# Attention on one core: VectorE's work for the compressed branch and the choice of blocks, one operation to a step over two units

## The chip, the core and the metric

The kernel runs on one core of a Trainium2 chip. The metric is the time of one execution of the whole program on the device, in microseconds (us). It is run several times and the median is taken; one further execution is recorded by the hardware profiler, and all durations below come from that one. Five engines work side by side, each through its own queue in order: PE (TensorE, matrix products, with its weight loads shown apart as PEld), DVE (VectorE), ACT (ScalarE), POOL (GpSimd) and SP (SyncE, which issues most DMAs). They wait for each other through semaphores.

## What is computed

The reference is a two-layer decoder trunk in float32 over 1024 tokens of 1024 features: a pooling mixer and a dense SwiGLU, then shared keys and values, an attention layer, and a mixture of experts. The change is in the attention alone. Its queries are taken in blocks of 128, for 16 heads in 4 groups that share keys. Each query attends three times, and the three results are added with gates:

```python
s = einsum(qblk, k_cmp) + bias          # compressed: 63 summaries of 32 keys, every 16
p_cmp = masked_softmax(s, dc >= 0)
o_cmp = einsum(p_cmp, v_cmp)
imp = einsum(p_cmp, cmp_to_slc)         # summed over a group's 4 heads: worth of each of 16 key blocks
score = where(forced, FORCED_SCORE, where(valid, imp, NEG))
_, sel = lax.top_k(score, 4)            # selected branch: the 4 best blocks of 64 keys
...                                     # window branch: the last 256 keys
return g0 * o_cmp + g1 * o_slc + g2 * o_win
```

So the compressed branch has to be done for a block of queries before the selected branch of that block can begin, because it chooses the blocks.

## The kernel before, in words

The program is a chain of phases; `attend` is one of them, and runs from about 1380 to 1895 us of the profile. Its work is cut into 8 **tiles** `i` of 128 queries, each tile into 4 **units** `u = 4 * i + g` (one for each group of heads `g`), and each unit into 8 **steps** `b` (written b0 to b7 below). Even steps are the selected branch of one of the group's 4 heads, over the `(i + 1) * 128` keys so far; odd steps are the window branch of the same head, over up to 384 keys. Nothing in the order is decided by a scheduler: each engine's program is written out by hand as loops over tiles, units and steps, and the engines meet at semaphores.

**PE** goes through `order`. For each step it makes the scores (`scores`, L1805, into one of two PSUM tiles `s_ps`, named att_s in the trace); then it does one part of the values of the unit before: `transpose_p` (L1828, L1831) turns the weights p, and `values` (L1847) multiplies them with v. `part` shares a unit's key tiles out over b2 to b7: **b0 and b1 have none**, b2 has at most one, the later ones have one or two. The part of a step comes after the scores of the step that follows. Since there are two score tiles, PE may make the scores of step n only when DVE has read those of step n - 2 (`free_scores`, on `s_sread`).

**DVE** reads each step's scores with the bias and the running minimum (`add_bias`: L1745 and L1750 in even steps of tiles 2 to 7, L1740 otherwise; att_neg_max is its result), and after each odd step makes two scale factors (`scale_of`, L1653, L1654) and weighs one window (`scale_win`, L1660). Between these stands its work for the **next** tile's compressed branch, which is all of what the change moves: `cmp_bias` (L1670) four times in unit g = 1, `cmp_max` (L1676, L1677), `cmp_scale` (L1682 to L1691), `block_scores` (L1696 to L1701) and `select_blocks` (L1709 to L1716). The places where they stand are these lines, in the body of the loop over steps:

```python
if g == 1 and b == 7:
    cmp_max(i + 1)
if g == 2 and b == 1:
    cmp_scale(i + 1)
if g == 2 and b == 4 and i + 1 >= 2:
    block_scores(i + 1)
if g == 2 and b == 6 and i + 1 >= 2:
    select_blocks(i + 1)
```

**ACT** takes the exponential of each step's scores (L1626), weighs the heads 0 and 2 of the selected branch (L1592), copies what PE has turned out of PSUM (`copy_pt`, L1586), and takes the exponential of the compressed branch (`exp_cmp`, L1608). **POOL** weighs the heads 1 and 3 (`scale_odd`, L1557), weighs the compressed branch (`scale_cmp`, L1535), and adds the choice of blocks to the bias of the two newest key tiles (`near_bias`, L1547, of which DVE's L1750 is the reader).

In the trace the tile `p_cmp` is called shared for even tiles and att_p_cmp for odd ones; `shares` is called shared too. A unit is said to start where DVE starts reading its first scores: units 2, 6, 10, 14, 18, 22 and 26 (g = 2 of tiles 0 to 6) start at 1397.69, 1442.79, 1493.25, 1552.10, 1617.27, 1689.68 and 1771.93 us.

Of the kernel before, what the change touches and what calls it, by code (L numbers as in the profile page):

```python
# [1412 lines left out]
def attend(nc, qkv, kt_dram, qt, load_q, s_q, kt, kct, vc, gates, win, cmpb, sel_const, row_valid, ident, ot_dram, first_sum, shared,  # L1413
# [12 lines left out]
    with ExitStack() as ctx:  # L1426
# [105 lines left out]
        def _(pool):  # L1532
# [27 lines left out]
            for u in range(4 * TILES):  # L1560
                i, g = divmod(u, 4)
                if u == 8:
                    near_bias(u, 0)
                    near_bias(u, 1)
                if u:
                    scale_odd(u - 1, 3)
                if g == 2 and i + 1 < TILES:
                    scale_cmp(i + 1)
                if u >= 8:
                    near_bias(u, 2)  # L1570
                    near_bias(u, 3)
                scale_odd(u, 1)
                if u >= 8 and u + 1 < 4 * TILES:
                    near_bias(u + 1, 0)
                    near_bias(u + 1, 1)
# [3 lines left out]
        def _(act):  # L1579
# [31 lines left out]
            for i in range(TILES):  # L1611
                for g in range(N_KV):
                    u = 4 * i + g
                    if g == 2 and i + 1 < TILES:
                        exp_cmp(i + 1)
                    for b in range(8):
                        k = 8 * u + b
                        if b % 2 == 0:
                            p = p_slc[u % 2][:, b // 2, 0:(i + 1) * P]
                        else:  # L1620
                            p = p_win[u % 2][:, b // 2, max(0, 2 - i) * P:3 * P]
                        act.wait_ge(s_sread, unit_step(u, b) + 1)
                        if k >= 8:

                            act.wait_ge(s_scale, k // 2 - 3)
                        act.activation(p, p, ACT.Exp, scale=-1.0, bias=neg_max[:, k % 8:k % 8 + 1],  # L1626
                                       accum_out=sums[:, k % 8:k % 8 + 1]).then_inc(s_exp, 1)
                        if b % 4 == 3:
                            scale_even(k - 3)
                        if u:  # L1630
                            values_part(u - 1, b)
# [5 lines left out]
        def _(dve):  # L1637
# [35 lines left out]
            def cmp_max(i):  # L1673
                pc = p_cmp[i % 2]
                dve.wait_ge(s_sread, cmp_step(i, 3) + 1)
                chain.step(dve.tensor_reduce(c_min[:, :], pc[:, :, :], AX.X, ALU.min))  # L1676
                dve.tensor_tensor(pc[:, :, :], pc[:, :, :], bc(c_min[:, :], NBL), ALU.subtract).then_inc(s_cready, 1)  # L1677

            def cmp_scale(i):
                pc = p_cmp[i % 2]  # L1680
                dve.wait_ge(s_cexp, i + 1)
                chain.step(dve.tensor_reduce(c_rs[:, :], pc[:, :, :], AX.X, ALU.add))  # L1682
                chain.step(dve.reciprocal(c_rs[:, :], c_rs[:, :]))
                if i == 0:

                    chain.step(dve.tensor_scalar(c_rs[:, :], c_rs[:, :], valid[:, 0:1], None, ALU.mult))
                if i >= 2:
                    chain.step(dve.tensor_tensor(shares[:, :, :], pc[:, :, :], bc(c_rs[:, :], NBL), ALU.mult))

                    dve.wait_ge(s_cscaled, i - 1)  # L1690
                dve.tensor_tensor(c_scale[i % 2][:, :], c_rs[:, :],  # L1691
# [61 lines left out]
            for g in range(N_KV):  # L1753
                cmp_bias(0, g)
            cmp_max(0)
            cmp_scale(0)
            for i in range(TILES):
                for g in range(N_KV):
                    u = 4 * i + g
                    for b in range(8):  # L1760
# [4 lines left out]
                        if i + 1 < TILES:  # L1765
                            if g == 1 and b % 2:
                                cmp_bias(i + 1, b // 2)
                            if g == 1 and b == 7:
                                cmp_max(i + 1)
                            if g == 2 and b == 1:  # L1770
                                cmp_scale(i + 1)
                            if g == 2 and b == 4 and i + 1 >= 2:
                                block_scores(i + 1)
                            if g == 2 and b == 6 and i + 1 >= 2:
                                select_blocks(i + 1)
            scale_of(8 * 4 * TILES - 2)
            scale_win(8 * 4 * TILES - 1)
# [775 lines left out]
```

## Time and profile before

| what | value |
|---|---|
| median of 3 runs | 4199.45 us (4198.1 to 4200.04) |
| the profiled execution, its own time | 4201.67 us |
| its span in the profile | 4200.1 us |
| PE busy, share of the span | 96% |
| DVE, ACT, POOL busy | 56%, 39%, 10% |
| mean granted clock of PE | 0.973 of full speed |

The span is the time between the first and the last record, so the profiled execution's own time is a little longer. Shares of busy time are means over all phases; what a change inside the attention is worth is read from the attention's own stretch, from the idle time of its engines and from what ended it. In rows of the timeline the number in square brackets is how long the engine sat idle before the row, and behind it stands what released it.

### The profile page before, as it was taken

The numbers are of one execution on the slowest core, as the hardware profiler recorded it, in microseconds if no ns is written. First come the engines' busy times: TensorE is split into PE (matmuls) and PEld (weight loads), VectorE is DVE, ScalarE is ACT, GpSimd is POOL, SyncE is SP. The second block draws the span as 40 slices with busy tenths as digits, with TensorE's granted clock in tenths as the row PEclk, the third lists the DMA queues.
The fourth block names the chain that finished last, engine by engine and source line by source line (L and its number), as shares of the span: only waits on it lengthen the run. The fifth ranks groups of instructions, "written<-read, shape, count | busy, mean of one in ns | idle before, by whom it ended". The sixth has DMA issues, their size and how long they took to land.

```text
span 4200.1 us, 63442 instructions
## 1 busy us (share of the span) xinstructions
PE 4015.1 (96%) x23002; PEld 3464.3 (82%) x23002; DVE 2363.0 (56%) x3482; ACT 1631.3 (39%) x2260; POOL 423.9 (10%) x439
## 2 busy tenths in 40 slices
PE   8999999998998899998699999999999999999998
PEld 6888888886887556556599999999999999999987
DVE  4444444445443676652455555555566666666678
ACT  3222222223342577673232332333334444444455
POOL 2000000000231243340100010010010100101010
PEclk8999999998999799999799999999999999999999
DMA  5222232233544211004333343344354545555567
GB/s 218 100 91 109 100 130 90 90 110 138 170 146 137 87 40 45 22 17 154 144 146 127 133 160 120 146 151 150 140 187 180 204 180 200 186 192 211 190 251 266
DMA packets 153671, 594.27 MB, mean 141 GB/s; under 512 B 26896, under 2 KB 54928, under 8 KB 113043
## 3 DMA queue, kind: packets, MB, share of 16 engines
q1 hardware_dynamic: 139076, 548.02, 36.1%
q0 software_dynamic: 10384, 35.14, 3.0%
q10 hardware_dynamic: 4080, 9.44, 0.6%
q8 instruction: 73, 1.20, 0.1%
q14 instruction: 58, 0.48, 0.0%
HBM read 535.76 MB, written 57.83 MB: 141 GB/s over the span
## 4 chain that ended last, share of the span: by engine, by line
PE 49%; DVE 1%; issue 0%; ACT 0%; DMA 0%; POOL 0%; DVEq 0%; POOLq 0%; ACTq 0%
PE moe_ps L443 10%; PE moe_ps L445 10%; PE moe_ps L444 10%; PE moe_ps L485 5%; PE moe_ps L486 5%; PE moe_ps L487 5%; PE moe_ps L424 1%; PE moe_ps L452 1%; PE moe_ps L453 1%; PE moe_ps L456 1%; DVE moe_yacc L364 0%; DMA moe_stage<-h_moe,moe_ids 0%; DVE moe_ht_lo L323 0%; PE moe_ps L458 0%; DVE moe_wd_lo L352 0%
## 5 line engine op out<-in xcount | busy, mean ns | idle before, releaser
L443 PE MATMUL moe_ps<-moe_ht_hi,moe_gu_hi 128*128 128x256 f32 (+4 forms) x3136 | 936.6, 299 | 1.6 <-DVE moe_ht_lo L323 1.6
L445 PE MATMUL moe_ps<-moe_ht_hi,moe_gu_lo 128*128 128x256 f32 (+4 forms) x3136 | 936.1, 298 | 0.0
L444 PE MATMUL moe_ps<-moe_ht_lo,moe_gu_hi 128*128 128x256 f32 (+4 forms) x3136 | 935.6, 298 | 0.0
L244 ACT CAST moe_gu_hi<-moe_gu_raw 128x2048 fp32r<-128x2048 f32 x226 | 431.0, 1907 | 521.3 <-PE moe_ps L445 487.8
L327 DVE TENSOR_TENSOR moe_gu_lo<-moe_gu_raw,moe_gu_hi 128x2048 fp32r<-128x2048 f32 x226 | 517.3, 2289 | 170.3 <-ACT moe_gu_hi L244 168.8
L443 PEld LDWEIGHTS moe_ps<-moe_ht_hi,moe_gu_hi 128*128 128x128 f32 x3136 | 596.2, 190 | 5.4 <-issue 1.8
L444 PEld LDWEIGHTS moe_ps<-moe_ht_lo,moe_gu_hi 128*128 128x128 f32 x3136 | 597.0, 190 | 3.5
L445 PEld LDWEIGHTS moe_ps<-moe_ht_hi,moe_gu_lo 128*128 128x128 f32 x3136 | 596.0, 190 | 0.0
L364 DVE SCALAR_TENSOR_TENSOR moe_yacc<-moe_ps,job_weights,moe_yacc 128x512 f32<-128x512 f32 x504 | 374.9, 750 | 326.8 <-PE moe_ps L487 326.8
L485 PE MATMUL moe_ps<-moe_wd_hi,moe_hid_hi 128*128 128x512 f32 x1008 | 395.8, 393 | 0.0
L486 PE MATMUL moe_ps<-moe_wd_lo,moe_hid_hi 128*128 128x512 f32 x1008 | 393.4, 390 | 0.0
L487 PE MATMUL moe_ps<-moe_wd_hi,moe_hid_lo 128*128 128x512 f32 x1008 | 392.9, 390 | 0.0
L443 PE MATMUL ffn_ps<-ffn_ht_hi,ffn_gu_hi 128*128 128x512 f32 x896 | 349.9, 391 | 1.6 <-DVE ffn_ht_lo L323 1.6
L444 PE MATMUL ffn_ps<-ffn_ht_lo,ffn_gu_hi 128*128 128x512 f32 x896 | 349.7, 390 | 0.0
L445 PE MATMUL ffn_ps<-ffn_ht_hi,ffn_gu_lo 128*128 128x512 f32 x896 | 349.5, 390 | 0.0
L367 DVE TENSOR_TENSOR ffn_yacc<-ffn_yacc,ffn_ps 128x512 f32<-128x512 f32 x224 | 153.8, 689 | 255.1 <-PE ffn_ps L487 254.9
L269 ACT CAST moe_hid_hi<-moe_hid 128x256 fp32r<-128x256 f32 (+4 forms) x196 | 84.9, 433 | 506.6 <-DVE moe_hid L342 506.6
L352 DVE TENSOR_TENSOR moe_wd_lo<-moe_wd_raw,moe_wd_hi 128x2048 fp32r<-128x2048 f32 x112 | 255.8, 2284 | 1.8 <-ACT moe_wd_hi L276 1.8
L342 DVE TENSOR_TENSOR moe_hid<-moe_act_gate,moe_ps 128x256 f32<-128x256 f32 (+5 forms) x224 | 96.9, 432 | 259.5 <-PE moe_ps L445 258.2
L2427 POOL DMA_INDIRECT out_x<-moe_yacc,job_to x18 | 28.8, 1597 | 1955.1 <-DVE moe_yacc L364 1955.1
L487 PEld LDWEIGHTS moe_ps<-moe_wd_hi,moe_hid_lo 128*128 128x128 f32 x1008 | 189.4, 188 | 40.3
L485 PEld LDWEIGHTS moe_ps<-moe_wd_hi,moe_hid_hi 128*128 128x128 f32 x1008 | 189.9, 188 | 37.2 <-DVE moe_yacc L364 1.1
(355 smaller groups left out, 6627.2 us busy)
## 6 DMA issues: line engine op xcount, KB each, us to landing
moe_gu_raw<-in_moe_wgu SPq DMA_DIRECT2D x228, 1024.0 KB, 4.9
moe_wd_raw<-in_moe_wd SPq DMA_DIRECT2D x112, 1024.0 KB, 6.7
first_gu<-in_ffn_wgu SPq DMA_DIRECT2D x58, 1024.0 KB, 4.8
ffn_wd_raw<-in_ffn_wd SPq DMA_DIRECT2D x28, 1024.0 KB, 6.8
kvq_lo<-qt SPq DMA_DIRECT2D x8, 1024.0 KB, 4.8
kt<-kt_rows SPq DMA_DIRECT2D x8, 1024.0 KB, 6.5
shared<-in_w_kvq SPq DMA_DIRECT2D x5, 1024.0 KB, 7.8
kvq_raw<-in_w_kvq SPq DMA_DIRECT2D x5, 1024.0 KB
```

The lines of the kernel that those rows point to most:

```text
L244: act.copy(gu_hi[s][:, :, :, :].rearrange("p a k c -> p (a k c)"), gu_raw[r][:, :]).then_inc(s_gu_hi, 1)
L327: dve.tensor_tensor(gu_lo[s][:, :, :, :].rearrange("p a k c -> p (a k c)"), gu_raw[r][:, :], gu_hi[s][:, :, :, :].rearrange("p a k c -> p ...
L342: dve.tensor_tensor(hid[s][:, 0:W], act_gate[s][:, 0:W], gate_ps[s][:, W:2 * W] if W == P else up_ps[s][:, 0:W], ALU.mult).then_inc(s_hid, 1)
L352: dve.tensor_tensor(wd_lo[b][:, :, :], wd_raw[b][:, :, :], wd_hi[b][:, :, :], ALU.subtract).then_inc(s_wd_lo, 1)
L364: dve.scalar_tensor_tensor(out=part, in0=y_ps[u % 4][:, :], scalar=row_weights[1][:, t:t + 1], in1=part, op0=ALU.mult, op1=ALU.add).then_i ...
L367: dve.tensor_tensor(part, part, y_ps[u % 4][:, :], ALU.add).then_inc(s_yadded, unit)
L443: pe.matmul(out[:, 0:W], gu_hi[s][:, half, k, :], ht_hi[:, k, 0:W], start=(k == 0), stop=False)
L444: pe.matmul(out[:, 0:W], gu_hi[s][:, half, k, :], ht_lo[:, k, 0:W], start=False, stop=False)
L445: last = pe.matmul(out[:, 0:W], gu_lo[s][:, half, k, :], ht_hi[:, k, 0:W], start=False, stop=(k == KT - 1))
L485: pe.matmul(out, hid_hi[b][:, a, rows], wd_hi[b][:, a, cols], start=(a == 0), stop=False)
L486: pe.matmul(out, hid_hi[b][:, a, rows], wd_lo[b][:, a, cols], start=False, stop=False)
L487: last = pe.matmul(out, hid_lo[b][:, a, rows], wd_hi[b][:, a, cols], start=False, stop=(a == GROUP - 1))
```

## The change

The number of operations stays the same. On DVE the old `cmp_max` is split into `cmp_max` (minimum) and `cmp_center` (subtraction), the old `cmp_scale` into `cmp_sums`, `cmp_shares` and `cmp_scale`, and the pieces stand at other steps of units g = 2 and g = 3. On ACT the exponential of the compressed branch stands ahead of b4 of unit g = 2 where it stood ahead of b0. On POOL its weighing stands in unit g = 3, behind `scale_odd(u, 1)`, where it stood in unit g = 2 behind `scale_odd(u - 1, 3)`.

```diff
--- before.py
+++ after.py
@@ -1564,12 +1564,12 @@
                     near_bias(u, 1)
                 if u:
                     scale_odd(u - 1, 3)
-                if g == 2 and i + 1 < TILES:
-                    scale_cmp(i + 1)
                 if u >= 8:
                     near_bias(u, 2)
                     near_bias(u, 3)
                 scale_odd(u, 1)
+                if g == 3 and i + 1 < TILES:
+                    scale_cmp(i + 1)
                 if u >= 8 and u + 1 < 4 * TILES:
                     near_bias(u + 1, 0)
                     near_bias(u + 1, 1)
@@ -1611,10 +1611,10 @@
             for i in range(TILES):
                 for g in range(N_KV):
                     u = 4 * i + g
-                    if g == 2 and i + 1 < TILES:
-                        exp_cmp(i + 1)
                     for b in range(8):
                         k = 8 * u + b
+                        if g == 2 and b == 4 and i + 1 < TILES:
+                            exp_cmp(i + 1)
                         if b % 2 == 0:
                             p = p_slc[u % 2][:, b // 2, 0:(i + 1) * P]
                         else:
@@ -1674,18 +1674,24 @@
                 pc = p_cmp[i % 2]
                 dve.wait_ge(s_sread, cmp_step(i, 3) + 1)
                 chain.step(dve.tensor_reduce(c_min[:, :], pc[:, :, :], AX.X, ALU.min))
+
+            def cmp_center(i):
+                pc = p_cmp[i % 2]
                 dve.tensor_tensor(pc[:, :, :], pc[:, :, :], bc(c_min[:, :], NBL), ALU.subtract).then_inc(s_cready, 1)
 
-            def cmp_scale(i):
-                pc = p_cmp[i % 2]
+            def cmp_sums(i):
                 dve.wait_ge(s_cexp, i + 1)
-                chain.step(dve.tensor_reduce(c_rs[:, :], pc[:, :, :], AX.X, ALU.add))
+                chain.step(dve.tensor_reduce(c_rs[:, :], p_cmp[i % 2][:, :, :], AX.X, ALU.add))
                 chain.step(dve.reciprocal(c_rs[:, :], c_rs[:, :]))
                 if i == 0:
 
                     chain.step(dve.tensor_scalar(c_rs[:, :], c_rs[:, :], valid[:, 0:1], None, ALU.mult))
+
+            def cmp_shares(i):
+                chain.step(dve.tensor_tensor(shares[:, :, :], p_cmp[i % 2][:, :, :], bc(c_rs[:, :], NBL), ALU.mult))
+
+            def cmp_scale(i):
                 if i >= 2:
-                    chain.step(dve.tensor_tensor(shares[:, :, :], pc[:, :, :], bc(c_rs[:, :], NBL), ALU.mult))
 
                     dve.wait_ge(s_cscaled, i - 1)
                 dve.tensor_tensor(c_scale[i % 2][:, :], c_rs[:, :],
@@ -1753,6 +1759,8 @@
             for g in range(N_KV):
                 cmp_bias(0, g)
             cmp_max(0)
+            cmp_center(0)
+            cmp_sums(0)
             cmp_scale(0)
             for i in range(TILES):
                 for g in range(N_KV):
@@ -1768,10 +1776,16 @@
                             if g == 1 and b == 7:
                                 cmp_max(i + 1)
                             if g == 2 and b == 1:
+                                cmp_center(i + 1)
+                            if g == 2 and b == 5:
+                                cmp_sums(i + 1)
+                            if g == 2 and b == 7 and i + 1 >= 2:
+                                cmp_shares(i + 1)
+                            if g == 3 and b == 0:
                                 cmp_scale(i + 1)
-                            if g == 2 and b == 4 and i + 1 >= 2:
+                            if g == 3 and b == 1 and i + 1 >= 2:
                                 block_scores(i + 1)
-                            if g == 2 and b == 6 and i + 1 >= 2:
+                            if g == 3 and b == 3 and i + 1 >= 2:
                                 select_blocks(i + 1)
             scale_of(8 * 4 * TILES - 2)
             scale_win(8 * 4 * TILES - 1)
```

The first place is DVE in unit 26 (tile 6, g = 2), from the end of b1 to the start of b2. Before:

```order
L1654 TENSOR_TENSOR att_scale<-gates,att_sums 128x2
L1660 TENSOR_SCALAR att_p_win1<-att_p_win1,att_scale 128x384
L1682 TENSOR_REDUCE att_c_rs<-att_p_cmp1 128x16
L1683 RECIPROCAL att_c_rs<-att_c_rs 128x16
L1688 TENSOR_TENSOR shared<-att_p_cmp1,att_c_rs 128x1024
L1691 TENSOR_TENSOR att_c_scale1<-att_c_rs,gates 128x16
L1745 ISA att_p_slc0,att_far_min<-att_sel0,att_s0 128x640
```

After the change (new line numbers: L1680 is `cmp_center`, L1751, L1756 and L1746 are the reads of `add_bias`):

```order
L1653 RECIPROCAL att_sums<-att_sums 128x2
L1654 TENSOR_TENSOR att_scale<-gates,att_sums 128x2
L1660 TENSOR_SCALAR att_p_win1<-att_p_win1,att_scale 128x384
L1680 TENSOR_TENSOR att_p_cmp1<-att_p_cmp1,att_c_min 128x1024
L1751 ISA att_p_slc0,att_far_min<-att_sel0,att_s0 128x640
```

Four operations stood between b1 and b2; now the subtraction alone stands there, which was in unit 25.

The second place is DVE in unit 27 (tile 6, g = 3), from the end of b0 to the start of b2. Before:

```order
L1750 ISA att_p_slc1,att_neg_max<-att_near0,att_s0,att_far_min 128x256
L1750 ISA att_neg_max 128x1
L1740 ISA att_p_win1,att_neg_max<-win,att_s1 128x384
L1740 ISA att_neg_max 128x1
L1653 RECIPROCAL att_sums<-att_sums 128x2
L1654 TENSOR_TENSOR att_scale<-gates,att_sums 128x2
L1660 TENSOR_SCALAR att_p_win0<-att_p_win0,att_scale 128x384
L1745 ISA att_p_slc1,att_far_min<-att_sel0,att_s0 128x640
```

After the change (L1697 is `cmp_scale`, L1702 to L1707 are `block_scores`):

```order
L1697 TENSOR_TENSOR att_c_scale1<-att_c_rs,gates 128x16
L1746 ISA att_p_win1,att_neg_max<-win,att_s1 128x384
L1746 ISA att_neg_max 128x1
L1653 RECIPROCAL att_sums<-att_sums 128x2
L1654 TENSOR_TENSOR att_scale<-gates,att_sums 128x2
L1660 TENSOR_SCALAR att_p_win0<-att_p_win0,att_scale 128x384
L1702 TENSOR_REDUCE att_group_p<-shared 128x256
L1704 TENSOR_REDUCE att_imp<-att_group_p 128x64
L1705 SCALAR_TENSOR_TENSOR att_imp<-att_group_p,att_imp 128x64
L1707 SCALAR_TENSOR_TENSOR att_imp<-att_group_p,att_imp 128x4x15
L1751 ISA att_p_slc1,att_far_min<-att_sel0,att_s0 128x640
```

Unit 27 held no work for the compressed branch; now one small product stands between b0 and b1, and the four operations of `block_scores` between b1 and b2. `select_blocks` follows behind b3.

The third place is POOL around its weighing of tile 7's compressed branch. Before:

```order
L1547 TENSOR_TENSOR att_near1<-win,att_sel0 128x256
L1557 TENSOR_SCALAR att_p_slc1<-att_p_slc1,att_scale 128x896
L1535 TENSOR_TENSOR att_p_cmp1<-att_p_cmp1,att_c_scale1 128x1024
L1547 TENSOR_TENSOR att_near0<-win,att_sel0 128x256
L1547 TENSOR_TENSOR att_near1<-win,att_sel0 128x256
L1557 TENSOR_SCALAR att_p_slc0<-att_p_slc0,att_scale 128x896
```

After the change:

```order
L1547 TENSOR_TENSOR att_near1<-win,att_sel0 128x256
L1557 TENSOR_SCALAR att_p_slc1<-att_p_slc1,att_scale 128x896
L1535 TENSOR_TENSOR att_p_cmp1<-att_p_cmp1,att_c_scale1 128x1024
L1547 TENSOR_TENSOR att_near0<-win,att_sel1 128x256
L1547 TENSOR_TENSOR att_near1<-win,att_sel1 128x256
L1557 TENSOR_SCALAR att_p_slc1<-att_p_slc1,att_scale 128x896
```

The weighing now stands right ahead of the first two `near_bias` of unit 28, and behind unit 27's own first weighing, `scale_odd(27, 1)`.

## Rows read from the trace of the kernel before

**Rows 1.** The page of the profile, its parts 1 and 2.
```profile
PE 4015.1 (96%) x23002; PEld 3464.3 (82%) x23002; DVE 2363.0 (56%) x3482; ACT 1631.3 (39%) x2260; POOL 423.9 (10%) x439
...
PEclk8999999998999799999799999999999999999999
```

**Rows 2.** Waits of PE, 1386 to 1915 us: total, times, longest.
```profile
PE att_s L1805 <- DVE att_neg_max L1750: 24.4, 22, 2.9
```

**Rows 3.** Stretches (eight units): us, busy PE, PEld, DVE, ACT, POOL, granted clock, DMA.
```profile
1397.69:1408.53 10.84, 8.29 (x36) 5.51 (x38) 6.97 (x33) 6.48 (x23) 3.29 (x3) 0.54 0.05 14
...
1442.79:1457.08 14.29, 10.39 (x54) 6.45 (x54) 13.49 (x45) 8.08 (x24) 4.06 (x3) 0.76 0.03 9
1552.10:1569.80 17.70, 14.06 (x78) 8.17 (x78) 16.29 (x54) 11.26 (x26) 7.88 (x7) 0.90 0.03 8
1617.27:1636.97 19.70, 16.14 (x94) 9.98 (x95) 17.25 (x53) 13.25 (x29) 8.53 (x7) 0.91 0.03 8
1689.68:1714.05 24.37, 20.49 (x104) 12.14 (x102) 17.16 (x53) 14.78 (x30) 9.21 (x7) 0.79 0.02 6
1714.05:1731.17 17.12, 16.49 (x104) 10.09 (x104) 9.26 (x37) 13.30 (x30) 7.36 (x6) 1.00 0.20 70
1771.93:1793.74 21.81, 17.69 (x110) 10.71 (x110) 17.73 (x52) 14.99 (x31) 9.83 (x7) 1.00 0.02 7
1793.74:1812.81 19.07, 18.48 (x114) 11.01 (x112) 9.94 (x36) 14.76 (x31) 7.94 (x6) 1.00 0.03 9
```

**Rows 4.** Timeline of unit 26, steps 0 to 2: start, length in us.
```profile
1770.43 1.22 DVE L1677 TENSOR_TENSOR att_p_cmp<-att_p_cmp,att_c_min 128x1024 f32<-128x1024 f32 x1
...
1774.13 2.75 POOL L1557 TENSOR_SCALAR att_p_slc<-att_p_slc,att_scale 128x896 f32<-128x896 f32 x1 [6.93 <-DVE att_scale L1654]
...
1774.40 1.21 DVE L1682 TENSOR_REDUCE att_c_rs<-att_p_cmp 128x16 f32<-128x1024 f32 x1
...
1775.14 0.65 PE L1847 MATMUL att_o<-att_pt,first_sum 128*64 128x256 f32 x4
...
1775.94 1.22 DVE L1688 TENSOR_TENSOR shared<-att_p_cmp,att_c_rs 128x1024 f32<-128x1024 f32 x1
...
1777.31 0.82 DVE L1745 CUSTOM_DVE_ANT_0 att_p_slc<-att_sel,att_s 128x640 f32<-128x640 f32 x1
...
1778.72 1.08 PE L1805 MATMUL att_s<-kt,kvq_lo 128*128 128x512 f32 x4 [2.93 <-DVE att_neg_max L1750]
```

**Rows 5.** Timeline of unit 27, steps 1 to 3.
```profile
1796.96 0.65 PE L1847 MATMUL att_o<-att_pt,first_sum 128*64 128x256 f32 x4
...
1797.55 0.55 DVE L1740 CUSTOM_DVE_ANT_0 att_p_win<-win,att_s 128x384 f32<-128x384 f32 x1
...
1797.68 1.09 PE L1805 MATMUL att_s<-kt,kvq_lo 128*128 128x512 f32 x4
```

**Rows 6.** Timeline of unit 26, steps 4 to 7, VectorE.
```profile
1781.33 1.97 DVE L1696 TENSOR_REDUCE att_group_p<-shared 128x256 f32<-128x1024 f32 x1
...
1784.33 0.56 DVE L1740 CUSTOM_DVE_ANT_0 att_p_win<-win,att_s 128x384 f32<-128x384 f32 x1
...
1787.37 0.22 DVE L1709 TENSOR_TENSOR att_imp<-att_imp,att_consts 128x64 f32<-128x64 f32 x1
...
1789.78 0.56 DVE L1740 CUSTOM_DVE_ANT_0 att_p_win<-win,att_s 128x384 f32<-128x384 f32 x1
```

**Rows 7.** Timeline of PE in unit 2.
```profile
1400.91 0.69 PE L1805 MATMUL att_s<-kt,kvq_lo 128*128 128x128 f32 x2 [2.21 <-DVE att_neg_max L1740]
```

**Rows 8.** Timeline of PE in unit 6.
```profile
1443.26 0.84 PE L1805 MATMUL att_s<-kt,kvq_lo 128*128 128x256 f32 x4 [1.68 <-DVE att_neg_max L1740]
...
1447.53 0.79 PE L1805 MATMUL att_s<-kt,kvq_lo 128*128 128x256 f32 x2 [3.42 <-DVE att_neg_max L1740]
```

**Rows 9.** Timeline of PE in units 10 and 11.
```profile
1505.18 0.62 PE L1805 MATMUL att_s<-kt,kvq_lo 128*128 128x384 f32 x2 [1.43 <-DVE att_neg_max L1740]
...
1511.32 0.92 PE L1805 MATMUL att_s<-kt,kvq_lo 128*128 128x384 f32 x3 [0.84 <-DVE att_neg_max L1750]
```

## The prediction

> **What bounds the kernel now.** I read the page first: PE is busy for 96% of the span and DVE for 56% [rows 1], so a DVE operation costs time only where PE has nothing else to do. The attention is such a place. The list of PE's waits there shows that the largest is for DVE's reading of the scores: 24.4 us in 22 times, the longest 2.9 us [rows 2]. The busy time by stretch says in which units that is. In units 23 and 27 (g = 3) PE is busy for 16.49 of 17.12 and 18.48 of 19.07 us; in units 22 and 26 (g = 2) for 20.49 of 24.37 and 17.69 of 21.81 us [rows 3]. PE idles about 4 us in each unit g = 2 and about 0.6 us in its neighbour g = 3, and the extra is what the compressed branch costs.
>
> The timeline of unit 26 says why. Behind b1 DVE goes through four operations, from 1774.40 to 1777.31, so it reads b2 only after them. PE ends its one key tile of values at about 1775.8, and starts the scores of b4 at 1778.72 after 2.93 us of idling, released by that read [rows 4]. Yet before this the minimum and the subtraction (1.22 us, at 1770.43) stood ahead of b0, and behind b4 and b6 `block_scores` held DVE from 1781.33 to 1784.33 and `select_blocks` from 1787.37 to 1789.78 [rows 6], and PE's waits do not grow by them. **The place decides, not the size**: from b2 on PE has one or two key tiles of values between two scores, at b0 and b1 it has none, and DVE sets the pace. Unit 27 shows how little slack there is without any insertion: PE's last value product before the scores of b4 starts at 1796.96 and is over by 1797.6, DVE has read b2 when b3's read starts at 1797.55, and the scores of b4 start at 1797.68 [rows 5]. The two arrive within 0.1 us of each other, so whatever stands behind b1 goes wholly into PE's time.
>
> **The change part by part, tiles 3 to 6 (four times).** Behind b1 of g = 2 stood 2.91 us (1774.40 to 1777.31); now the subtraction alone stands there, 1.22 us and a gap, 1.25: minus 1.66. Taking it away from ahead of b0 gives at most 0.1, since DVE already finished it (1771.65) before the first read of unit 26 at 1771.93. The sums (1.21 and a reciprocal, about 1.5 us) behind b5 and the shares (1.22) behind b7 cost nothing: they are smaller than the 3.0 and 2.4 us that the same steps hid. If that cover were gone they would cost up to 2.7. The scale (2.91 - 1.25 - 1.21 = 0.45 is reciprocal and scale together, so about 0.2) now stands behind b0 of g = 3: 0 to 0.2, I take 0.1. **`block_scores`, 3.00 us, now stands behind b1 of g = 3**, the uncovered place, and goes in whole: plus 3.0. `select_blocks`, 2.4 us, behind b3 has key tiles beside it: 0 to 0.2, in these tiles with 8 or more key tiles. Together -1.66 - 0.1 + 0.1 + 3.0 + 0.1 = **+1.45 each, +5.8**.
>
> **Tiles 0 to 2.** Tile 0 (next tile 1 chooses no blocks): the 1.25 us leave a place where short units do wait, and behind b1 1.25 stands for 1.21 + 0.45 = 1.66: -1.65, against a wait of 2.21 us [rows 7]. Tile 1: PE waited 1.68 and 3.42 us [rows 8]; -1.25 - 1.66 in unit 6, +3.0 in unit 7, and `select_blocks` finds one key tile a step, about 1.5 us of PE for a step, so +0.5: +0.6. Tile 2: DVE is full in the old unit 10, so `block_scores` made PE wait another 1.43, and its backlog 0.84 in unit 11 [rows 9]. Both go, with 1.66 behind b1; 2.8 and, with one key tile a step against 1.2 + 2.7 + 0.7 of DVE, 1.5 come: +0.3. Sum of the work: -1.65 + 0.6 + 0.3 + 5.8 = **+5.05 us**.
>
> **The other engines.** ACT's exponential no longer waits at b0, and stands for about 1 us between copies ahead of b4's exponential. ACT idles over 6 us of unit 26 (14.99 busy of 21.81, [rows 3]), and the copies that it holds up are wanted one part later: 0, and 1 us a tile if that is wrong. On POOL the weighing now stands in front of `near_bias` for the next tile's first head, which DVE's L1756 at b0 waits for. POOL is busy for 9.83 us of unit 26 and 7.94 of unit 27, which has the same operations but this one [rows 3]: it takes 1.9 us, and unit 27 leaves POOL 11 us idle to put it in. In unit 7, half as long, room is short: 0, at worst 0.5. No DMA moves.
>
> **The granted clock** is the other term. It was at half speed for part of four of the six long waits: the clock of 0.76, 0.90, 0.91 and 0.79 in units 6, 14, 18 and 22 [rows 3] means (1 - clock) / 0.5 of their length, 6.9, 3.5, 3.5 and 10.2 us, at 1.2 GHz where the rest ran at 2.4; in unit 26 it did not fall. Half of these 24 us, 12, is the most it can cost; with PE idle in part of them I take 10. Unit 22 took 24.37 us though unit 26, with more keys, took 21.81. Each of the falls followed one of the long idle stretches. The change takes these stretches away (1.2 us remains) and makes six new ones of 3.0 to 3.5 us in g = 3. I take the same rate and price, four of six, 10 us: no difference. From both sides: no fall gives -10, six at the mean +5.
>
> The sum stands against the profiled execution's own time, 4201.67 (span 4200.1), which is 2.2 above the median; the difference carries over: 4199.45 + 5.05 = **4204.5 us**. A measurement of this kernel tells a change from none at about 0.2%, 8.4 us.
>
> **Rivals.**
>
> *A. The price of the new waits is the clock* (slower). Place: b1 to b4 of units 7, 11, ... 27. If it falls in all six it costs 15 instead of 10: 4209.5; as dearly as in unit 22 (5.1 each) 4225. It decides from 3.4 us more than I take. For it: a contiguous wait of 3.0 to 3.2 replaces 2.9, and 4 of 6 fell. Against: unit 26, 2.93 us, kept full speed. Chance 0.21.
>
> *B. There is cover behind b1 of g = 3* (faster). If PE's waits there are shorter than the insertion, or DVE, which no longer brings a backlog, runs ahead, the 6 x 3.0 us vanish: 4199.45 + 5.05 - 18 = 4186.5. For it: DVE idles more than half of unit 27 by busy time (9.94 of 19.07). Against: that idle time lies at b3 to b7, and the arrival within 0.1 us in [rows 5]. Also on this side: with shorter waits in unit 2 the clock, at 0.54 there [rows 3], stays up through unit 3, up to 8 us. Chance of both together 0.10.
>
> *C. The subtraction is held up by POOL* (slower). `scale_odd(u - 1, 3)` starts on POOL at 1774.13 and lasts 2.75 us, and the subtraction will now start at 1774.40 in the middle of it. If a DVE product of two SBUF tiles had to wait for POOL's end, that would add 2.5 us in tile 6, less with fewer keys, some 10 over all: 4214.5. Against it, in the same rows: L1688, a product with two SBUF inputs, started at 1775.94 with 0.94 us of that POOL operation to go, and took 1.22 us like the subtraction at 1770.43 with POOL idle [rows 4]. Chance 0.04. The Trainium skill speaks for this rival ("SBUF — State Buffer", section "Who interferes with whom"): a VectorE instruction with two SBUF inputs contends with a GpSimd instruction that reads SBUF, and whichever comes second is blocked for the whole of the other. By that rule the time would be the 4214.5 of this paragraph, and by the row it stays 4204.5; for this pair of operations the trace does not agree with it.
>
> *D. Forecast*, within 0.2%: 0.65.
>
> **How the numbers follow.** Faster by over 0.2% is B, 0.10; slower A and C, 0.25; the rest 0.65. The range goes from no falls (4194.5) to A with a fall in all six and a few us of errors in the small tiles, 4213; C and the dear end of A lie above it, B below.
>
> **What the profile after would show.** PE's wait at the scores of b4: about 1.2 in units 6 to 26 (g = 2), 3.0 to 3.2 in units 7 to 27, released by DVE's read of b2. Units 26 and 27 together 1.5 us longer than 40.88, at full clock. The subtraction at 1.22 us (else C). DVE at b0 of units 8, 12, ... not released by `near_bias`. Granted clock below 1.00 moves from g = 2 to g = 3. I am wrong if PE's waits in g = 3 are well under 3 us, if the stretches at half clock differ from 24 us by much, or if POOL or ACT shows up as a releaser in front of PE.

## The result, and the profile after

| | median, us | lowest to highest |
|---|---|---|
| kernel before (7 runs) | 4198.1 | 4195.09 to 4201.84 |
| changed kernel (7 runs) | 4215.27 | 4205.2 to 4218.53 |

The ratio is 1.0038, with an interval from 1.0028 to 1.0047: 16 us slower by it, between 12 and 20. The forecast was 4204.5 with a range to 4213; the time lies above it, where rival A stands. The profiled execution of the changed kernel took 4205.2 us (span 4202.8), which is the fastest of the seven, 10 us under their median. Its trace is read first, and the 10 us are looked for below.

The page of the changed kernel, against [rows 1]:

```profile
PE 4011.3 (95%) x23002; PEld 3462.1 (82%) x23002; DVE 2357.4 (56%) x3482; ACT 1629.6 (39%) x2260; POOL 430.4 (10%) x439
...
PEclk9999999999999899999799999999999999999999
```

The waits of PE from 1386 to 1925 us (total, times, longest), against [rows 2]:

```profile
PE att_s L1819 <- DVE att_neg_max L1756: 30.0, 26, 3.3
...
PE att_s L1819 <- DVE att_neg_max L1746: 10.4, 11, 3.4
```

The first line was 24.4 us in 22 times; the second, which [rows 2] doesn't show, was 11.6 us in 9. Together the waits grew from 36.0 to 40.4 us. That is 4.4 us more, about the size of the forecast's work sum, and not 16 us.

The stretches, against [rows 3]: units 2 and 3, then 6 and 7, 18 and 19, 22 and 23, 26 and 27 (us, busy PE, PEld, DVE, ACT, POOL, granted clock, DMA):

```profile
1395.91:1403.99 8.08, 5.24 (x38) 3.57 (x38) 6.53 (x32) 6.12 (x23) 2.44 (x2) 1.00 0.05 16
1403.99:1411.35 7.36, 6.60 (x46) 4.12 (x42) 5.17 (x30) 5.85 (x23) 3.27 (x3) 1.00 0.07 19
1430.89:1442.56 11.67, 9.63 (x54) 5.80 (x54) 9.08 (x33) 8.71 (x25) 3.22 (x2) 0.85 0.04 11
1442.56:1456.12 13.56, 10.00 (x58) 6.19 (x56) 10.84 (x42) 7.88 (x25) 5.18 (x5) 0.87 0.11 25
...
1610.47:1627.00 16.53, 14.65 (x96) 8.98 (x94) 12.66 (x41) 12.93 (x29) 7.74 (x6) 1.00 0.03 9
1627.00:1649.62 22.62, 19.44 (x100) 11.80 (x96) 13.44 (x50) 12.66 (x29) 8.42 (x7) 0.77 0.14 45
1686.67:1704.92 18.25, 16.06 (x103) 9.73 (x102) 13.47 (x41) 14.01 (x30) 8.37 (x6) 1.00 0.03 9
1704.92:1729.39 24.47, 20.84 (x108) 12.56 (x104) 14.15 (x50) 13.88 (x30) 9.10 (x7) 0.79 0.14 49
1770.24:1790.37 20.13, 17.72 (x111) 10.71 (x110) 13.60 (x41) 15.21 (x31) 9.00 (x6) 1.00 0.03 7
1790.37:1816.49 26.12, 22.32 (x116) 13.43 (x112) 14.71 (x50) 15.06 (x31) 9.70 (x7) 0.80 0.02 6
```

From tile 3 on the units g = 2 keep the full clock, and they are shorter than before: 18.25 for 24.37, 20.13 for 21.81. The units g = 3 carry the loss. By (1 - clock) / 0.5 of their length units 19, 23 and 27 spent 10.4, 10.3 and 10.4 us at 1.2 GHz, where before only unit 22 had spent 10.2. From unit 6 on the time at half clock is about 48 us by the same formula (units 11 and 15, not shown above, had 0.81 and 0.90), where the forecast counted on 24 in both kernels. Unit 27 shows it best: PE idles 3.80 us in it, and it is busy for 22.32 us with the same products that took 18.48 us in [rows 3].

Unit 27 of the changed kernel from b1 to the parts behind b4, against [rows 5]:

```profile
1792.86 1.94 DVE L1702 TENSOR_REDUCE att_group_p<-shared 128x256 f32<-128x1024 f32 x1
...
1793.51 0.65 PE L1861 MATMUL att_o<-att_pt,first_sum 128*64 128x256 f32 x4
...
1796.02 0.82 DVE L1751 CUSTOM_DVE_ANT_0 att_p_slc<-att_sel,att_s 128x640 f32<-128x640 f32 x1
...
1797.43 1.86 PE L1819 MATMUL att_s<-kt,kvq_lo 128*128 128x512 f32 x4 [3.27 <-DVE att_neg_max L1756]
...
1799.09 1.06 PE L1845 MATMUL att_t<-ident,att_p_win 128*128 128x128 f32 x4
1800.07 1.12 PE L1861 MATMUL att_o<-att_pt,first_sum 128*64 128x256 f32 x4
```

`block_scores` starts at 1792.86, and DVE reads b2 at 1796.02. PE has finished its one key tile by 1794.2 and waits 3.27 us for that read. Then the same value product that took 0.65 us at 1793.51 takes 1.12 us.

Unit 26 of the changed kernel, steps 1 to 4, against [rows 4]:

```profile
1772.36 3.80 POOL L1557 TENSOR_SCALAR att_p_slc<-att_p_slc,att_scale 128x896 f32<-128x896 f32 x1 [7.03 <-DVE att_scale L1654]
...
1772.63 1.22 DVE L1680 TENSOR_TENSOR att_p_cmp<-att_p_cmp,att_c_min 128x1024 f32<-128x1024 f32 x1
...
1775.17 1.09 PE L1819 MATMUL att_s<-kt,kvq_lo 128*128 128x512 f32 x4 [1.13 <-DVE att_neg_max L1756]
```

The subtraction kept its 1.22 us inside POOL's operation, and PE waits 1.13 us where it waited 2.93. POOL's operation is the one that grew, from 2.75 to 3.80.

### The profile page after: what moved, and what is told of

The parts are those of the page before. It is cut to its first block, busy times and chain, and to the rows that moved or that the text cites. A ratio compares the mean times of both kernels' runs of the same rounds, so it can differ in the third digit from the quotient of the medians.

```text
span 4202.8 us, 63449 instructions
## 1 busy us (share of the span) xinstructions
PE 4011.3 (95%) x23002; PEld 3462.1 (82%) x23002; DVE 2357.4 (56%) x3482; ACT 1629.6 (39%) x2260; POOL 430.4 (10%) x439
## 4 chain that ended last, share of the span: by engine, by line
PE 49%; DVE 1%; DMA 0%; issue 0%; ACT 0%; POOL 0%; DVEq 0%; POOLq 0%; SPq 0%; ACTq 0%
PE moe_ps L443 10%; PE moe_ps L445 10%; PE moe_ps L444 10%; PE moe_ps L485 5%; PE moe_ps L486 5%; PE moe_ps L487 5%; PE moe_ps L424 1%; PE moe_ps L452 1%; PE moe_ps L453 0%; PE moe_ps L456 0%; DMA moe_wd_raw<-in_moe_wd 0%; DVE moe_yacc L364 0%; DMA moe_stage<-h_moe,moe_ids 0%; DVE moe_gu_lo L327 0%; DVE moe_ht_lo L323 0%
```

## The experiments

Two theories stood against each other behind the result. One: the loss is the granted clock, which falls after the waits of 3 us that `block_scores` makes behind b1 of g = 3. The other: work that found no cover costs more than the sum said. Durations of units in this table run from VectorE's first read to the next unit's; the columns are the kernels by the names below.

```
unit  before  changed  e4     e6     e3     e7     e1     e8
 7     9.29   13.56   13.62   8.82  14.19  13.69  12.82  12.03
11    11.65   17.73   15.59  11.65  18.79  17.06  15.57  14.86
15    13.60   17.81   17.09  13.43  17.94  17.05  16.13  15.71
19    15.36   22.62   18.39  15.37  18.36  17.96  16.00  16.03
22    24.37   18.26   18.26  20.28  17.13  18.26  18.26  17.12
23    17.12   24.47   20.36  17.12  21.67  20.51  17.21  17.22
26    21.81   20.13   20.14  21.81  19.07  20.14  20.14  19.07
27    19.07   26.12   22.29  19.07  23.48  22.30  19.10  19.09
```

**e1_scores_b4: the changed kernel, with `block_scores` and `select_blocks` at covered steps of the same unit.**

```diff
-if g == 3 and b == 1 and i + 1 >= 2:
+if g == 3 and b == 4 and i + 1 >= 2:
     block_scores(i + 1)
-if g == 3 and b == 3 and i + 1 >= 2:
+if g == 3 and b == 6 and i + 1 >= 2:
     select_blocks(i + 1)
```

> The changed kernel with only block_scores moved from behind b1 to behind b4 of unit g = 3, and select_blocks from behind b3 to behind b6. Theory (the new waits of 3.0 to 3.3 us behind b1 of g = 3, and the half-speed clock that follows each of them, are the whole loss): PE's waits of 3 us in units 7 to 27 vanish (6 x 3.0 = 18 us), and with them the falls of the clock (15 to 20 us), so about 4180 us, faster than both kernels. Rival (the 3 us of DVE work cost PE the same wherever they stand, since DVE only carries the backlog on): about 4213, waits of PE at later steps of units 7 to 27.

4193.94 us, 0.9987 of before [0.9978, 0.9996], 21 us below the changed kernel. Unit 27 of this kernel:

```profile
1787.67:1806.77 19.10, 18.36 (x114) 10.95 (x112) 16.54 (x49) 14.65 (x31) 9.81 (x7) 1.00 0.03 9
```

VectorE is busy for 16.54 of the 19.10 us, and yet the unit is as long as before, when it held none of this work (19.07). So the loss of units 23 and 27 hangs on the steps at which these two pieces stand. `cmp_scale` and POOL's weighing stand in this unit at their new places too, and cost nothing either. That the time stays 14 us above the 4180 hoped for comes from the small tiles: unit 7 and 11 are still 12.82 and 15.57 us, and units 8, 12 and 16 were 12.32, 13.53 and 16.85 us long for 10.50, 12.21 and 14.14 before, in part at half clock. In these tiles PE still waits for VectorE at the last steps, 2.1 us once in unit 7, 1.0 and 1.2 in unit 11 and 1.0 in unit 15.

**e2_only_scores_moved: the kernel before, with these two pieces alone at b1 and b3 of g = 3.**

```diff
-if g == 2 and b == 4 and i + 1 >= 2:
+if g == 3 and b == 1 and i + 1 >= 2:
     block_scores(i + 1)
-if g == 2 and b == 6 and i + 1 >= 2:
+if g == 3 and b == 3 and i + 1 >= 2:
     select_blocks(i + 1)
```

> The kernel before with one part of the change alone: block_scores behind b1 and select_blocks behind b3 of unit g = 3 (from b4 and b6 of g = 2). The four operations behind b1 of g = 2 stay. Theory: PE waits 2.9 us in every g = 2 and 3.0 us in every g = 3 and the clock falls behind many of both: about 4228 us, against the changed kernel's 4215. Rival (the loss of the change comes from its other parts, on ACT or POOL or by the splitting): about the time of before, 4198, or at most plus the 18 us of the waits, 4216.

4224.94 us, 1.0067 [1.0053, 1.008]. Units 22, 23 and 27 of it:

```profile
1704.51:1727.26 22.75, 18.87 (x103) 11.25 (x103) 12.50 (x40) 14.12 (x30) 9.21 (x7) 0.85 0.02 7
1727.26:1751.35 24.09, 20.66 (x106) 12.43 (x108) 14.06 (x48) 13.98 (x30) 7.24 (x6) 0.79 0.14 50
...
1813.93:1837.35 23.42, 19.81 (x114) 11.99 (x116) 14.62 (x48) 15.12 (x31) 7.88 (x6) 0.93 0.03 7
```

Both waits stand here, 2.9 us in units 22 and 26 and 3.2 in units 23 and 27, and the clock falls at both in units 22 and 23, but not in unit 26. The moved pieces alone cost 27 us; the rest of the change gives 10 of them back.

**e3_center_back: the changed kernel, with the subtraction where it was, in unit g = 1.**

```diff
 cmp_max(i + 1)
-if g == 2 and b == 1:
-    cmp_center(i + 1)
+cmp_center(i + 1)
```

> The changed kernel with the subtraction (cmp_center) back in its old place, behind cmp_max at b7 of g = 1, instead of behind b1 of g = 2. Theory: the 1.1 us wait of PE in each unit g = 2 vanishes in tiles 1 to 6; tiles 0 and 1 wait 1.2 more at b0: about -6 us, 4209; the 3 us waits in g = 3 and their clock stay. Rival (the 1.1 us waits also help to bring the clock down): -15 us, 4200.

4199.37 us, 1.0001 [0.9992, 1.001]: 16 us less than the changed kernel, though this takes away only six waits of 1.1 us. Units 19, 23 and 27, and PE at the scores of b4 in unit 27:

```profile
1635.41:1653.77 18.36, 15.19 (x98) 9.30 (x96) 14.09 (x50) 12.31 (x29) 8.43 (x7) 1.00 0.17 55
1708.24:1729.91 21.67, 18.04 (x106) 11.05 (x104) 14.80 (x50) 13.70 (x30) 9.06 (x7) 0.92 0.16 56
1789.74:1813.22 23.48, 19.68 (x114) 11.88 (x112) 14.71 (x50) 14.86 (x31) 9.71 (x7) 0.93 0.02 7
```
```profile
1796.68 1.67 PE L1818 MATMUL att_s<-kt,kvq_lo 128*128 128x512 f32 x4 [3.27 <-DVE att_neg_max L1756]
```

The wait is the same 3.27 us, but the stretches at half clock are 3.5 and 3.3 us in units 23 and 27 instead of 10.3 and 10.4, and there is none in unit 19. In unit 11 it went the other way, 18.79 us for 17.73. The expectation that priced the waits alone (4209) is refuted, and its rival (4200) gave the time. Units 22 and 26 are also as long as before's 23 and 27 (17.13 and 19.07), which held no work of the compressed branch: sums, reciprocal, shares and ACT's exponential at their new places cost nothing.

**e4_filler: the changed kernel, with 16 products of the identity on PE ahead of the scores of b4 in units 7, 11, ... 27.** They fill about 2 of the 3.3 us in which PE waits; their output is overwritten and read by nobody.

```diff
+def filler(u):
+    m = part(u - 1, 3).start
+    pe.wait_ge(s_pt, m - 1)
+    for r in range(16):
+        pe.transpose(t_ps[m % 2][:, r % R, :], ident, ident)
...
+if x % 4 == 3 and 4 < x < 4 * (TILES - 1) and y == 4:
+    filler(x)
 scores(x, y)
```

> The changed kernel with 16 extra transposes of the identity (about 2.4 us of PE, into a PSUM tile that is free then) ahead of the scores of b4 in units 7, 11, ... 27, that is inside the 3 us waits. They do no useful work and should fit in the wait. Theory (much of the loss is the half-speed clock after the waits): the waits shrink to under 1 us of idleness, the clock stays up behind them, and the kernel gets 15 to 20 us faster than the changed one, about 4198, though PE has more to do. Rival (the clock is not what costs): no faster than 4215, or slower by what of the 2.4 us does not fit.

4197.86 us, 1.0003 [0.9994, 1.0012]. VectorE's order is the changed kernel's. PE in unit 27, and the stretches of units 19, 23 and 27:

```profile
1790.04 1.97 PE L1876 MATMUL att_t<-ident 128*128 128x128 f32 x16
1793.41 1.09 PE L1819 MATMUL att_s<-kt,kvq_lo 128*128 128x512 f32 x4 [1.40 <-DVE att_neg_max L1756]
```
```profile
1631.16:1649.55 18.39, 17.09 (x114) 11.03 (x112) 14.12 (x49) 12.30 (x29) 8.43 (x7) 1.00 0.16 55
1704.87:1725.23 20.36, 18.63 (x122) 11.82 (x120) 14.44 (x49) 13.53 (x30) 9.17 (x7) 1.00 0.16 59
1786.23:1808.52 22.29, 20.27 (x130) 12.73 (x128) 14.80 (x49) 14.72 (x31) 9.72 (x7) 1.00 0.03 7
```

More work on PE, and 17.4 us less time against the same kernel before (4215.27 - 4198.1, less 4197.86 - 4198.06). The clock stays up in these units, and they get 4.23, 4.11 and 3.83 us shorter. This is what the falls cost the changed kernel. The idle time that is left behind the filler is 1.40 us, not under 1 as expected, and the clock stays up with it.

**e6_before_filler: the kernel before with the same filler in its units 6, 10, ... 26** (`x % 4 == 2` in the condition).

> The kernel before with the 16 extra transposes of the identity (2.4 us of PE) ahead of the scores of b4 in units 6, 10, ... 26, that is inside its 2.9 us waits of g = 2. It measures what the clock cost the kernel before. My forecast's term (10 us): 4188. Rival (the falls of the kernel before were short and cost little; what they cost was overstated): 4195 to 4198.

4189.38 us beside 4196.89, 0.998 [0.9971, 0.9989]. Unit 22:

```profile
1680.23:1700.51 20.28, 18.29 (x121) 11.51 (x119) 17.41 (x53) 14.53 (x30) 9.16 (x7) 1.00 0.03 8
```

The falls of before cost 7.5 us by the medians. By the traces unit 22 has 4.09 of it (24.37 - 20.28), unit 18 1.5 and units 7, 14 and 15 together 1.1, which is 6.7; the same sum for the changed kernel and e4 is 15.0, where their medians gave 17.4. This also gives what the change costs as work, with the clock up on both sides: -0.2 for e4 less -7.5 for e6, both against their own runs of before, is 7.3 us. The 7.5 is the weaker of these numbers. The eleven times of e6 run from 4182.35 to 4198.29; six lie at 4182 to 4189 with mean clocks of 0.979 to 0.981, the other five at 4191 to 4198 with 0.975 to 0.978 (its 24 runs of before have 0.973 to 0.976), and the trace, one of the six, has a start of the attention at a higher clock that the trace of before has not (see e10). The sums by traces leave this start out.

**e5_both_covered: e1 and e3 together**, no piece behind b1 at all.

> The changed kernel with both steps that stood in an uncovered place moved: the subtraction back behind cmp_max at b7 of g = 1, block_scores behind b4 and select_blocks behind b6 of g = 3. The two single moves gave 4199.4 and 4193.9 against 4215.3. Theory (waits add, clock falls only behind long idle stretches): 7 us of waits less than with block_scores moved alone, so about 4187, and no half-speed stretch in tiles 3 to 6. Rival (the single moves each already gave back the same clock): 4193.

4187.1 us beside 4196.89, 0.9973 [0.9962, 0.9983]. Units 26 and 27 are 19.08 and 19.09 us, and no unit from 19 to 27 shows a clock below 1.00. Against runs of before the two edits together are worth 27 us to the changed kernel (17.2 above it to 9.8 below), less than the 21.3 and 15.9 that they gave one by one: either alone already takes away most of the time at half clock in these units.

**e7_sums_b1_rest_b3: the changed kernel, with only the first operation of `block_scores` (1.94 us) behind b1**, the other three with `select_blocks` behind b3.

```diff
 if g == 3 and b == 1 and i + 1 >= 2:
-    block_scores(i + 1)
+    group_sums(i + 1)      # its first tensor_reduce
 if g == 3 and b == 3 and i + 1 >= 2:
+    block_scores(i + 1)    # the other three
     select_blocks(i + 1)
```

> The changed kernel with only the first operation of block_scores (1.94 us) left behind b1 of g = 3; its other three (1.0 us) stand with select_blocks behind b3. So the wait of PE behind b1 shrinks from 3.0 to about 2.0 us. Theory (the clock answers to how much PE idles at a stretch): beside 6 us of waits the half-speed stretches of tiles 4 to 6 go too, about 12 us: 4198. Rival (each wait at this place brings the clock down whatever its length): 4209.

4198.8 us beside 4196.89, 1.0003 [0.9993, 1.0012]. Unit 27, and PE's wait in it:

```profile
1791.43:1813.73 22.30, 19.70 (x114) 11.93 (x112) 14.44 (x50) 14.98 (x31) 9.69 (x7) 0.92 0.03 7
```
```profile
1797.31 1.36 PE L1821 MATMUL att_s<-kt,kvq_lo 128*128 128x512 f32 x4 [2.07 <-DVE att_neg_max L1757]
```

The wait is 1.2 us shorter than the changed kernel's, the unit 3.8 us. Of the 15.3 us saved against runs of before (17.2 to 1.9) at most 7 are six such waits; what is left falls to the clock, at half speed for 3.6 us of this unit (0.08 / 0.5 of 22.30) and for 10.4 in the changed kernel.

**e9_center_back_filler: e3 with the filler of e4.**

> center_back (the subtraction back at b7 of g = 1, 4199.4 us) with the 16 extra transposes in its 3 us waits of g = 3. Putting the subtraction back alone gave 16 us where its waits are worth 7. If the other 9 us are clock, center_back must itself lose less to the clock than the changed kernel does (which got 17.4 us from the same filler): theory: this gives only 7 to 9 us, 4191. Rival (the subtraction behind b1 costs 16 us of its own, in something else than waits and clock): the filler gives 17 us again, 4182.

4190.38 us beside 4198.82, 0.9975 [0.9964, 0.9986]. e3 stood 1.3 us above its runs of before and this one 8.4 below, so the filler gives 9.7 us here, against 17.4 in e4. With the clock held up in both, taking the subtraction back is worth 8.2 us (-0.2 to -8.4). The other 7.7 of e3's 15.9 are then less time at half clock in units g = 3, as the traces show it for units 19, 23 and 27.

**e8_spread: e5, with `block_scores` and `select_blocks` cut in two each**, at b3, b4, b5 and b6 of g = 3 (`select_rest` is the last four operations of `select_blocks`).

```diff
+if g == 3 and b == 3 and i + 1 >= 2:
+    group_sums(i + 1)
 if g == 3 and b == 4 and i + 1 >= 2:
     block_scores(i + 1)
-if g == 3 and b == 6 and i + 1 >= 2:
+if g == 3 and b == 5 and i + 1 >= 2:
     select_blocks(i + 1)
+if g == 3 and b == 6 and i + 1 >= 2:
+    select_rest(i + 1)
```

> As both_covered, but block_scores and select_blocks are cut in four pieces behind b3 (the sum over the group's heads, 1.94 us), b4 (the rest of block_scores, 1.0 us), b5 and b6 (four small operations each, 1.2 us) of g = 3. Theory (in tiles 1 to 3 a step has one key tile of values, about 1.5 us of PE, and can hide no more than that less DVE's own reads, so pieces of 3.0 and 2.4 us still make PE wait there, 2 to 4 us a tile): 5 us faster than both_covered, about 4182. Rival (DVE as a whole is full in these units, so that cutting changes nothing): the same as both_covered.

4183.66 us beside 4196.89, 0.9962 [0.9949, 0.9976]: the fastest, 13 us under the kernel before. In the whole of unit 27 PE waits for VectorE once:

```profile
PE att_s L1829 <- DVE att_neg_max L1763: 0.5, 1, 0.5
```

The 3.4 us that it is below e5 are not clear of the noise (its five times run from 4176.44 to 4190.25, and the two intervals overlap). The small tiles still pay: unit 7 is 12.03 us for 9.29 before, unit 11 14.86 for 11.65.

**e10_changed_again: the changed kernel once more, one execution**, to see why the profiled one had been 10 us faster than the median.

> The changed kernel once more, one profiled execution, to see what of its clock record belongs to the program and what to the execution. Theory: the waits of PE in every unit repeat within 0.1 us, the half-speed stretches behind the 3 us waits are there again in all six units but with other lengths, and the half-speed stretch of about 27 us in units 2 to 4, absent in the first record, is likely to be back. Rival: the record repeats as it is, with units 2 to 4 at full speed, and then the first trace stands for the median of 4215 only by 10 us that nothing explains.

4211.7 us. Units 2, 3, 4, and 19, 23 and 27:

```profile
1392.54:1402.68 10.14, 8.31 (x36) 5.54 (x38) 6.70 (x32) 6.49 (x23) 2.44 (x2) 0.59 0.04 13
1402.68:1413.11 10.43, 10.32 (x42) 6.59 (x42) 4.26 (x30) 6.02 (x23) 3.26 (x3) 0.50 0.08 19
1413.11:1423.35 10.24, 10.01 (x44) 6.01 (x42) 5.32 (x29) 6.27 (x20) 1.78 (x2) 0.58 0.26 102
1634.35:1656.96 22.61, 19.45 (x98) 11.82 (x96) 13.40 (x50) 12.65 (x29) 8.41 (x7) 0.77 0.13 43
1712.28:1736.75 24.47, 20.84 (x106) 12.57 (x104) 14.16 (x50) 13.87 (x30) 9.10 (x7) 0.79 0.15 49
1797.76:1823.87 26.11, 22.32 (x114) 13.42 (x112) 14.72 (x50) 15.06 (x31) 9.70 (x7) 0.80 0.02 6
```

The last three units repeat the first trace to 0.01 us; that the falls would come back with other lengths is refuted for them. Units 2 to 4 do not repeat: 30.8 us here at about half clock, 21.9 in the first trace (8.08, 7.36 and 6.44). Units 6 and 7 don't either: 12.89 and 14.22 us at 0.74 and 0.76, where the first trace had 11.67 and 13.56 at 0.85 and 0.87. The trace of before had 30.9 in units 2 to 4 (10.83, 10.43 and 9.64). So the first trace of the changed kernel had a lucky start of the attention, worth 9 us there and 2 more in units 6 and 7. Units 0 to 30 together took 493.7 us before, 497.8 in the first trace and 508.5 here: 14.8 us more than before where both have the slow start, which is most of the 16. The traces of e2 and e6 have a start at full clock in units 3 and 4 too, those of the other seven experiments do not. What decides it was not tested; it may be part of the 7.5 us of e6.

## Why the prediction was wrong

**What failed is the clock's term**: "I take the same rate and price, four of six, 10 us: no difference". Rival A took its place. The clock was below 1.00 in all six units g = 3 (the traces of units 11 and 15 had 0.81 and 0.90), and the falls of units 19, 23 and 27 were each as long as the one of unit 22 before. The filler prices the term on both sides: 17.4 us in the changed kernel and 7.5 in the kernel before, so the term was +9.9 and not 0, with some 7 us of uncertainty from the intervals of the runs (+8.3 by the units of the traces). With the 2.3 us by which the same runs put the work sum too low (below) this makes up the way from +5.05 to +17.2. For before I had taken 10, near enough; it was the rate and the length at the new waits that did not carry over.

I had argued from two things about one wait, its idle time and whether the clock fell at it. The runs show that this is too little. Waits of nearly one size stood beside 10.2, 6.8, 3.4 or 0 us at half clock, and what differs with the length is the moment of the fall (by windows cut finely around it, which give 10.2 us for the 10.3 and 10.4 that the clock of two digits gave above):

```
                  unit  PE's wait  the clock fell          then at half clock for
before            18    2.79       0.4 us behind its end    3.4 us
before            22    2.92       0.6 us ahead of its end  10.2 us
before            26    2.93       it did not
changed (twice)   27    3.27       0.9 us ahead of its end  10.2 us
e3                19    2.91       it did not
e3                27    3.27       0.3 us behind its end    3.4 us
e2                22    2.92       1.3 us behind its end    6.8 us
e2                27    3.19       0.6 us behind its end    3.4 us
e7                27    2.07       0.6 us behind its end    3.4 us
```

The traces of before, of the changed kernel (two), of e2 and of e3 have 30 such waits of 2.7 to 3.3 us in units 10 to 27. In the 11 where the clock fell 0.5 us or more ahead of the wait's end it stayed at half for 10.2 us, each time; in 15 it fell later and stayed for 3.4 or 6.8; in 4 it did not fall. What stands in the unit ahead can't be the whole of it, since units 18, 22 and 26 of the kernel before have the same operations ahead of them and differ. So waits of one size cost nothing or 4 us, and the length at half clock goes with where the fall comes in them. What sets this moment is open: no run moved it alone, and e10 could not test it, since its falls came at the same places in the units as those of the first trace (6.17 for 6.19 us behind the start of unit 27). Whether the gains of e3 and e7 come from less idle time or from another moment of the fall is therefore not shown.

**The place decides, not the size**: right. Six waits of 2.8 to 3.4 us appeared in units 7 to 27, where 3.0 to 3.2 were forecast, and e1, which moved two pieces to other steps of the same unit, made units 23 and 27 as short as before.

**The work sum, +5.05**: 7.3 measured with the clock held up, with some 4 us of uncertainty on each of its two sides, so that the 2.3 more are not clear of noise in the medians. (The terms written for one of tiles 3 to 6 add up to 1.44 and those of tile 2 to 0.37, not 1.45 and 0.3; this changes the sum by under 0.1.) By units of the traces of e4 and e6, tiles 3 to 6 (units g = 1 to 3 of each) cost 1.5, 1.4, 1.3 and 1.7 us for the 1.45 forecast; units 26 and 27 together 42.43 for 40.88, which is the 1.5 named. Tile 2 gave 0.4 instead of costing 0.3. Tile 0 can't be read, since the clock differs at its start. Tile 1 was mis-sized: 2.3 for 0.6. Its unit 7 grew by 4.8 us, where 3.0 for `block_scores` and 0.5 for `select_blocks` were put; part of this is again time at half clock, since e4's trace shows some of it there.

**Subtraction behind b1, sums behind b5, shares behind b7, scale behind b0**: right. PE waits 1.13 us at the scores of b4 in unit 26, where 1.2 were forecast, e3's unit 26 shows sums and shares at no cost, and e1's unit 27 the scale.

**ACT and POOL**: right. POOL shows up nowhere as a releaser in front of PE, ACT in two waits of 0.5 us together (before, in one of 0.2), and VectorE at b0 of units 8, 12, ... 28 waits for PE's transposes, not for `near_bias`.

**Rival B** had two halves. The cover behind b1 of g = 3 isn't there. The clock in units 2 and 3 did stay up, but in one of two executions, and in the traces of e2 and e6, which keep the old order in unit 2, it stayed up in unit 3 too: this is no effect of the change.

**Rival C** fell, but the two engines do get in each other's way, the other way round; see below.

## What to carry to other kernels

Where two engines meet in every step, put inserted work where the waiting engine has other work of its own, and cut it small: in unit 27 5.4 us of VectorE's work cost 7 us behind b1 and b3 (4 of them clock) and nothing at b3 to b6; in units half as long they still cost 3. Before moving an idle stretch of PE from one place to another, don't carry its price over: the same wait of 3.3 us stood beside 3.3 or 10.4 us at half clock. And price the clock by experiment: a few products without a use in the wait show how much of the time is clock and how much is work.

## What the runs showed of the hardware

**The falls of the clock repeat.** In two executions of one kernel units 19, 23 and 27 had the same length to 0.01 us with 0.77, 0.79 and 0.80 in both, although they started 7 us apart in the two spans. Units 2 to 4, 6 and 7 differed. In both executions the falls came at the same places in these units, so this does not tell what sets them. A fall of 10.3 to 10.4 us cost 3.83 to 4.23 us of time (the changed kernel less e4). The Trainium skill ("TensorE: Matmul & The Clock Gate", section "HAM oscillation — how this bites in real kernels") prices the time throttled at half its length. By that rule these falls would cost an estimated 5.2 us each. The runs give about three quarters of it; that PE also waits for others within such a stretch would explain it, and is not shown.

**VectorE's subtraction lengthens POOL's operation, not its own.** The 128x896 weighing of heads on POOL, x8 in the attention, in the changed kernel and then in e3, where the subtraction no longer starts inside it (columns at the end: total us and mean ns of one, then idle time ahead):

```profile
L1557 POOL TENSOR_SCALAR att_p_slc<-att_p_slc,att_scale 128x896 f32<-128x896 f32 x8 | 23.0, 2878 | 47.0 <-DVE att_scale L1654 47.0
```
```profile
L1557 POOL TENSOR_SCALAR att_p_slc<-att_p_slc,att_scale 128x896 f32<-128x896 f32 x8 | 22.0, 2749 | 44.2 <-DVE att_scale L1654 44.2
```

The 1.0 us more in eight is the one of unit 26, 3.80 for 2.75, so nearly the whole of the subtraction's 1.22 us. The same 1.05 to 1.06 us stands in all seven tiles, whatever the length of POOL's operation. It cost nothing, since POOL idles for 11 us of the unit. Not every overlap does this. In the kernel before the sum L1682, which reads one tile and takes 1.21 us, began at the same 0.27 us behind POOL's start, and POOL kept its 2.75 ([rows 4]); and the product L1688, which reads two tiles like the subtraction, overlapped the last 0.94 us of that operation, and neither grew. The Trainium skill ("SBUF — State Buffer", section "Who interferes with whom") says that such a pair excludes each other and that the one that comes second waits. That they exclude each other agrees with the 1.05 us of the subtraction, but not with L1688; that the second waits agrees with neither, since VectorE came second both times and lost nothing.
